# Two-block transformer kernel: second attention's first scores issued before the first attention's last value product, and the first attention's norm split between steps of the second

## The reference, cut to what matters

```
def diff_attention(...):        # group a: 4 heads, two softmaxes per head, head width 32 + 32
    s = einsum('bqhcd,bkhcd->bhcqk', q, k) * 32 ** -0.5      # keys: 512 tokens + 256 context
    p = softmax(s, axis=-1)
    a = p[:, :, 0] - lam * p[:, :, 1]
    o = einsum('bhqk,bkhd->bqhd', a, v)                      # value width 64
    return rmsnorm(o, subln_g) * (1.0 - lam_init)

def neighbourhood_attention(...):  # group b: 4 heads of width 64, one softmax
    s = concat([q @ k_window + bias, q @ k_ctx]) * 64 ** -0.5
    p = softmax(s, axis=-1)
    return p_win @ v_rows + p_ctx @ v_ctx

xl = xl + g1 * (concat([a, b, pool, hyena], axis=-1) @ w_out)   # w_out: 1024 x 1024
```

## Time and profile before

| | us |
|---|---|
| median of 3 runs | 1615.59 |
| lowest, highest | 1614.81, 1634.83 |
| the profiled execution, its own time | 1593.27 |
| its span, first to last instruction | 1591.4 |
| PE busy in the span | 1367.3 (86%) |
| DVE busy | 849.4 (53%) |
| ACT busy | 557.6 (35%) |
| POOL busy | 141.6 (9%) |
| mean granted TensorE clock | 0.892 of full speed |

### The profile page before, as it was taken

How to read it: one execution, slowest core, us unless ns; L and a number is a source line. 1 busy time by engine, 2 the same in 40 slices (tenths; PEclk the granted TensorE clock), 3 DMA queues, 4 the chain that set the end, 5 groups by cost and what they waited for, 6 DMA issues and landing times.

```text
span 1591.4 us, 16706 instructions
## 1 busy us (share of the span) xinstructions
PE 1367.3 (86%) x6328; PEld 947.2 (60%) x6328; DVE 849.4 (53%) x1316; ACT 557.6 (35%) x746; POOL 141.6 (9%) x129
## 2 busy tenths in 40 slices
PE   6999999888898961899999984699978877799986
PEld 2544476666685451688888863254456655568864
DVE  4169787377651144688888864400165455433333
ACT  1340102145342122577777852111133322532322
POOL 2001110001500002022111202000000000000000
PEclk9899999999699965999999986799977667899998
DMA  9425575630400041899999957113212211421211
GB/s 367 194 82 222 192 297 185 145 80 1 169 0 1 29 185 41 306 398 401 406 403 411 410 206 276 61 53 115 80 44 83 88 35 15 159 106 77 82 53 54
DMA packets 48454, 259.09 MB, mean 163 GB/s; under 512 B 14343, under 2 KB 21415, under 8 KB 35080
## 3 DMA queue, kind: packets, MB, share of 16 engines
q1 hardware_dynamic: 37048, 209.46, 35.3%
q0 software_dynamic: 8896, 39.87, 6.8%
q10 hardware_dynamic: 2448, 8.91, 1.4%
HBM read 223.09 MB, written 31.47 MB: 160 GB/s over the span
## 4 chain that ended last, share of the span: by engine, by line
PE 79%; DVE 11%; ACT 3%; DMA 3%; issue 3%; POOL 1%; SPq 0%; DVEq 0%; POOLq 0%; ACTq 0%
PE PS L2234 48%; PE PS L2587 6%; PE PS L2588 6%; PE PS L2589 6%; PE PS L2772 2%; PE PS L2665 2%; DMA ring<-in_slabs 1%; PE PS L2495 1%; PE PS L2251 1%; PE PS L2766 1%; PE PS L2581 1%; PE PS L2736 1%; DVE rstd L1473 1%; PE PS L2714 1%; DVE stat L1745 1%
## 5 line engine op out<-in xcount | busy, mean ns | idle before, releaser
L2234 PE MATMUL PS<-hT,ring 128*128 128x512 f32 (+1 forms) x704 | 294.3, 578 | 11.7 <-DVE hT L2027 10.3
L2234 PEld LDWEIGHTS PS<-hT,ring 128*128 128x128 f32 x704 | 134.0, 192 | 168.3 <-issue 152.5
L2234 PE MATMUL PS<-arena 128*128 128x64 f32 (+7 forms) x744 | 189.1, 404 | 26.4 <-DMA arena<-in_small_f_w 8.0
L1176 ACT ACTIVATE arena_r<-ring 128x2048 fp32r<-128x2048 f32 x102 | 189.4, 1910 | 12.3 <-ACT arena L1186 8.8
L2234 PEld LDWEIGHTS PS<-arena 128*128 128x128 f32 (+2 forms) x744 | 118.6, 205 | 82.8 <-issue 57.8
L1965 DVE TENSOR_TENSOR arena_r<-ring,arena_r 128x2048 fp32r<-128x2048 f32 x68 | 152.7, 2288 | 14.5 <-ACT arena_r L1176 14.3
L2234 PE MATMUL PS<-arena_r 128*128 128x512 f32 x384 | 134.5, 405 | 19.9 <-DVE ring_r L2143 10.6
L2587 PE MATMUL PS<-arena_r,hT_r 128*128 128x512 f32 x272 | 112.7, 414 | 10.8 <-DVE arena_r L1965 10.8
L2588 PE MATMUL PS<-arena_r,hT_r 128*128 128x512 f32 x272 | 108.5, 399 | 0.0
L1023 ACT ACTIVATE arena<-PS 128x1024 f32<-128x1024 f32 (+1 forms) x32 | 30.8, 970 | 221.6 <-PE PS L2234 213.7
L2234 PE MATMUL PS<-arena_r,ring_r 128*128 128x512 f32 x256 | 102.5, 400 | 0.0
(11 more groups left out here) (377 smaller groups left out, 2118.9 us busy)
## 6 DMA issues: line engine op xcount, KB each, us to landing
ring<-in_moe SPq DMA_DIRECT2D x51, 2048.0 KB, 10.1
ring<-in_slabs SPq DMA_DIRECT2D x32, 2048.0 KB, 11.8
y_rows<-arena ACTq DMA_DIRECT2D x17, 512.0 KB, 9.7
ssm_scratch<-arena POOLq DMA_DIRECT2D x4, 1152.0 KB, 5.6
arena<-ssm_scratch POOLq DMA_DIRECT2D x4, 1152.0 KB, 7.7
arena<-in_tab_fwd SPq DMA_DIRECT2D x2, 2048.0 KB, 15.3
ssm_scratch<-arena POOLq DMA_DIRECT2D x4, 1024.0 KB, 10.7
y_rows<-in_tab_no_token SPq DMA_DIRECT2D x1, 3584.0 KB, 20.8
```

The costliest lines, as they stand in the source:

```text
L1176: nc.scalar.activation(rounded(moe_w_hi[n][:, cols]), ring[:, n, cols], ACT.Copy).then_inc(s_moe_hi[n], 1)
L2234: ins = nc.tensor.matmul(out, lhsT, rhs, start=(n == 0), stop=(n == len(pairs) - 1))
```

## The change

The order of units: b's `s0` now comes between `t15` and `o15` of a (as turn `s_b`), and `ot_a` moves from i == 2 to i == 9 of b. The exponentials of b go to two separate regions; the even one is in a part of the convolution table that is free by then, so the exponential of s0 need not wait for o15. On DVE the row maximum of b's s0 stands before the scaling of a's o15, and `mean_a` and `norm_a` are cut into pieces which are done one at a time behind `output("b", i - 1)` for i = 2, 3, 5, 6 and 7. On ACT the square root moves from the seam to b's turn `o` of step 3. The computation is the same.

```diff
 def turns(a, n):
-    yield from [("s", 0, c) for c in range(2 if a == "a" else 1)]
+    yield from [("s", 0, c) for c in range({"a": 2, "b": 0, "g": 1}[a])]
     for i in range(n + 1):
         ahead, behind = i + 1 < n, i >= 1
         if behind:
             yield ("t", i - 1)
+        if a == "a" and i == n:
+            yield ("s_b", 0)
...
-        if a == "b" and i == 2:
+        if a == "b" and i == 9:
             yield ("ot_a",)
...
+    if kind == "s_b":
+        return ("b", "s", 0, 0), "act"
...
-        prob_b = region(R_QKV + 2560, [2, TC])
+        prob_b = [region(R_FWD + 4 * TC, [TC]), region(R_QKV + 2560, [TC])]
...
+                    elif turn[0] == "s_b":
+                        act.wait_ge(s_max, 2 * n + 1)
+                        nc.scalar.activation(prob_b[0], both(key)[:, 0:TC], ACT.Exp, bias=stat[:, 2 * n % 8, 0:1], scale=1.0,
+                                             accum_out=stat[:, 2 * n % 8, 1:2]).then_inc(s_act_read, 1)
...
                     elif turn[0] == "o":
                         if a == "a":
                             high_b(i)
+                        elif i == 3:
+                            root(3, o_root[:])
...
-                if a == "a":
-                    root(3, o_root[:])
-                else:
+                if a == "b":
                     out_tr(a, QT - 1)
...
-            def mean_a():
-            def norm_a():
+            def normed_a(step):
+                if step == 0:
+                    read(dve, ("a", "o", n - 1))
+                    then(nc.vector.tensor_tensor(o_a2, o_a, o_a, ALU.mult))
+                elif step == 1:
+                    then(nc.vector.tensor_reduce(o_root[:], ...))
+                    nc.vector.tensor_scalar(o_root[:], o_root[:], 1.0 / VD, EPS, ALU.mult, ALU.add).then_inc(s_mean, 1)
+                elif step == 3:
+                    inverse(3, o_root[:])
+                    then(nc.vector.tensor_scalar(o_root[:], o_root[:], 1.0 - LAM_INIT, None, ALU.mult))
+                elif step == 4:
+                    then(nc.vector.tensor_tensor(oh, oh, o_root[...], ALU.mult))
+                elif step == 5:
+                    nc.vector.tensor_tensor(oh, oh, R("subln")[...], ALU.mult).then_inc(s_o, 1)
...
+                if i == n:
+                    row_max("b", 0, 0, 2 * n)
                 if i >= 1:
                     output("a", i - 1)
             then(nc.vector.scalar_tensor_tensor(out=gain2[:], ...))
-            mean_a()
-            row_max("b", 0, 0, 2 * n)
             for i in range(n + 1):
                 if i + 1 < n:
                     row_max("b", i + 1, 0, 2 * n + i + 1)
                 if i >= 1:
                     output("b", i - 1)
-                if i == 0:
-                    norm_a()
+                if 2 <= i <= 7:
+                    normed_a(i - 2)
...
                     if turn[0] == "s":
                         scores(a, turn[1], turn[2])
+                    elif turn[0] == "s_b":
+                        scores("b", 0, 0)
```

More of the change, by code:

```diff
@@ L1113, in _ @@
                             filled(act, ("a", "o", n - 1))
-                        nc.scalar.activation(prob_a[:, i % 2, c] if a == "a" else prob_b[:, i % 2], both(key)[:, 0:TC], ACT.Exp,
+                        nc.scalar.activation(prob_a[:, i % 2, c] if a == "a" else prob_b[i % 2], both(key)[:, 0:TC], ACT.Exp,
                                              bias=stat[:, j % 8, 0:1], scale=1.0,
                                              accum_out=stat[:, j % 8, 1:2]).then_inc(s_act_read, 1)
+                    elif turn[0] == "s_b":
+                        act.wait_ge(s_max, 2 * n + 1)
+                        nc.scalar.activation(prob_b[0], both(key)[:, 0:TC], ACT.Exp, bias=stat[:, 2 * n % 8, 0:1], scale=1.0,
+                                             accum_out=stat[:, 2 * n % 8, 1:2]).then_inc(s_act_read, 1)
                     elif turn[0] == "t":
@@ L1778, in _ @@
             oh = o_a.rearrange("p a (b c) -> p (a b) c", b=HEADS)
-            def mean_a():
[L1782 to L1785, removed]
-            def norm_a():
[L1788 to L1792, removed]
+            def normed_a(step):
[3 more added lines that the diff above has]
+                elif step == 1:
+                    then(nc.vector.tensor_reduce(o_root[:], o_a2.rearrange("p a (b c) -> p (a b) c", b=HEADS), AX_X, ALU.add))
+                    nc.vector.tensor_scalar(o_root[:], o_root[:], 1.0 / VD, EPS, ALU.mult, ALU.add).then_inc(s_mean, 1)
[3 more added lines that the diff above has]
+                elif step == 4:
+                    then(nc.vector.tensor_tensor(oh, oh, o_root[:, :, None].broadcast_to([P, QT * HEADS, VD]), ALU.mult))
+                elif step == 5:
+                    nc.vector.tensor_tensor(oh, oh, R("subln")[:, None, :].broadcast_to([P, QT * HEADS, VD]),
+                                            ALU.mult).then_inc(s_o, 1)
             for c in range(2):
@@ L2492, in _ @@
                             read(pe, (a, "s", i, 0))
-                        p = prob_a[:, i % 2, 0] if a == "a" else prob_b[:, i % 2]
+                        p = prob_a[:, i % 2, 0] if a == "a" else prob_b[i % 2]
                         for t in range(KT):
```

## The result

The changed kernel took 1618.26 us (median of 20 runs, 1607.58 to 1634.46) against 1609.28 us before (20 runs, 1599.69 to 1634.83): ratio 1.0056, 95% interval 1.0032 to 1.008. It is slower, by 9 us in this comparison. A second one with fresh runs (experiment 6) gave 1.0112, 1.0075 to 1.0149. Both are inside 2%.

The account below looks back on a forecast made before the run. Bound by PE's 3.52 us hole where a meets b and a clock fallen to 0.50. Seven more low steps 18.5, slow ot unit +0.2, seam -3.6 checked +15.4 taken; on 1615.6 that gave 1631.0 us, range 1603 to 1651.

Parts of the forecast that it names:

- The seam: Where a meets b: scores s0 moved ahead close PE's hole, b's t0 at 423.6 instead of 427.20, gain 3.6 us.
- 0 (if s0 is late): Low end of the gain where a meets b: nothing gained if s0 comes late; the other end was 4.5 us.
- the norm in pieces: DVE pieces spread over b's steps: hidden at the low clock, 0.9 us at most shown at the high; taken as 0.
- Steps at the low clock and ot_a: b's first nine steps stay at 0.50 clock, 6.25 us each, until ot_a at 480.3; o9 15.3 us late.
- From there on units and clock are as before, 27.17 us: From b's o9 to wo, units and clock were to stay unchanged, taking 27.17 us.
- added to 1615.6 the difference gives 1631.0: Whole program: one profiled execution's difference, +15.4 us, added to the runs' median 1615.6 to forecast 1631.0 us.
- Late again: Rival, chance 0.14: ot_a at step 9 fails to lift the clock, steps 10 to 15 run low; 1649 us.
- Faster: Rival, chance 0.18: clock returns once PE has no hole, or never falls in most executions; -9.4 us, 1606.
- Early lift: Rival, chance 0.12: ot unit after o6 and t7's transposes return the clock about 13 us earlier; 1625.5 us.
- the change doesn't do what it says: Rival, chance 0.04: s0 is held back, the hole stays and ot_a is late all the same; 1634.6 us.
- The square root: ACT, steps 3 and 4 of b: about 2.8 us with table loads, hidden at low clock, 1.1 at high; taken 0.
- The rule of the Trainium skill: Keeping TensorE continuously busy brings the full clock, so the change would help doubly; the prediction set 12.50 us at 0.50 against it.

Follow-up runs that it names:

- experiment 6: Both kernels unchanged, measured again with fresh runs: changed kernel 1619.50 against 1602.46 us, ratio 1.0112; the kernel before against itself 1.0005.
- experiment 1: Changed kernel with the norm whole at the seam and ot_a at its old place, so only the scores moved ahead: ratio 1.0017 to the kernel before.
- experiment 2: Kernel before with one line changed, ot_a behind o8 instead of o1: ratio 1.0122 to the kernel before.
- experiment 4: Changed kernel with identity transposes filling PE's waits, in three growing sets: ratios 1.0062, 0.9943 and 0.9913 to the kernel before.
- experiment 4's second run: Changed kernel with 71 identity transposes in PE's long waits from the end of a to wo, o4 not included: ratio 0.9943 to the kernel before.
- the last run of experiment 4: Changed kernel with identity transposes in PE's long waits from the end of a to wo, o4 included: median 1588.91 us, ratio 0.9913 to the kernel before.
- experiment 3's first run: Changed kernel with 8 identity transposes ahead of t2's own, where ot_a stood before: ratio 1.0077 to the kernel before.

## Why the prediction was right or wrong

Point by point, counted from t14's start.

- **The seam: right.** t0 forecast at 13.6, found at 13.7. Its end of "0 (if s0 is late)" did not come. The sum gives the 3.6 to the scores and 0 to the norm in pieces; experiment 1 shows that the scores alone gain nothing, so the 3.6 belong to both together.
- **Steps at the low clock and ot_a: right.** 6.25 each; ot_a forecast at 70.3, found at 70.5; o9 forecast at 74.8, found at 75.2. The prediction's main claim, that b's steps do not bring the clock back and ot_a does, holds in all three profiles of the changed kernel, and experiment 2 makes it with one line. As a rule for every moment it is too strong: in experiment 4 the `ot` unit and t7, which are part of b's steps, did bring it back once.
- **"From there on units and clock are as before, 27.17 us": wrong, 31.2.** The waits in b's last steps were in the trace that I had, and at them the clock may fall or not: it fell there in all three profiles of the changed kernel, and in one of three of the kernel before. That is 4.1 us on the stage, and in the stage as in the second comparison the forecast of 15.4 was too small, not too large: 17 to 20.
- **The median: wrong.** The step that failed is the last one of the sum, "added to 1615.6 the difference gives 1631.0", in both of its terms. The base was the median of three runs. With 20 runs the kernel before has 1609.28, and on other occasions 1601.8 to 1605.1; so 6.3 of the 12.7 us by which 1631.0 missed 1618.26 are the base. The other 6.4 are the difference, 15.4 forecast and 9.0 found in the first comparison (its interval is 5 to 13 us). I had one execution's alignment and priced it as if each had it. In all three profiles of the changed kernel the seven low steps stand as they were priced, 6.25 each, and the second comparison gave 17.0. What pulls the first one to 9.0 stays open. The changed kernel is the same in both, in time (1618.26 and 1619.50) and in the mean granted clock of its timed executions (0.875 and 0.875); it is the kernel before that took 6.8 us more in the first. Its executions there have no clock on record. A rise missed behind ot_a in some of them would do that, and so would a difference between chips or occasions; no run shows either.
- **Rivals.** *Late again* did not occur in the stage: the clock came back behind ot_a each time, and its later fall at the end of b is another one. *Faster*, 0.18, did not occur by itself; made by force (experiment 4) it is real and larger than I had it, -12.7 on the stage instead of -9.4. *Early lift* did not occur in three profiles: the ot unit at step 7 with t7 behind it was not enough. It is no empty rival, though: that very pair lifted the clock in experiment 4's second run. That *the change doesn't do what it says* is out, t0 came as forecast.
- **The square root: right.** In the low steps it is hidden. At the high clock step 4 takes 4.87 us in the last run of experiment 4, beside 3.64 and 3.68: 1.2, forecast 1.1. The norm's pieces show by less than 0.3.
- **The rule of the Trainium skill** ("TensorE: Matmul & The Clock Gate", section "Why this matters for your kernels"), that continuous work brings the full clock, failed again and more plainly by this trace: 56.72 us without a gap at 0.50.

## What to carry to other kernels

Before a big-array unit is moved away from a run of small ones, look at the granted clock around it in the profile: the unit may be what brings the clock back, and its own 1.7 us are then the small part of its worth. A gain on waits at a low clock can be smaller than keeping the clock: here closing a hole gave 3.5 us, and filling seven waits with dead transposes on top of it gave 32 us on the stage. Difference and base are two estimates; three runs do not give a base to half a per cent when single executions spread over two, and one profile does not give a difference either.

## What the runs showed of the hardware that I had not expected

- **More work made the program faster.** 85 transposes of the identity took the changed kernel's stage from 106.4 to 74.0 us.
- **The same row of transposes lifts the clock or not.** 14 in a row lifted it in all three profiles of the kernel before, and not in experiment 3's first run, where 8 of them were of the identity. The 8 of the `ot` unit and t7 lifted it in one profiled execution of seven.
- **A tiny DVE instruction ends when POOL's instruction ends.** One `tensor_scalar` over 128x16 elements (the mean's scale, L1795) took 1.22 us in experiment 1, where POOL worked on the pooling sums beside it, and 0.17 us in the changed kernel, where it comes later and POOL is idle:

```profile
449.37 1.21 DVE L1794 TENSOR_REDUCE o_root<-arena 128x16 f32<-128x1024 f32 x1
450.61 0.17 DVE L1795 TENSOR_SCALAR o_root<-o_root 128x16 f32<-128x16 f32 x1
```

In experiment 1 it ended at 439.22 and POOL's instruction at 439.19. `gain2` ended at 435.45 there and POOL's at 435.44; in the kernel before, the mean's scale ended at 424.43 and the factor of 1.73 us at 429.55, beside POOL's ends of 424.40 and 429.51. The reduction over 128x1024 takes 1.22 and 1.21 with and without POOL, so not every DVE instruction is held. In the changed kernel the scale costs 0.36 us less than before (0.17 against 0.53), and 1.05 less than in experiment 1.
